# Loading the first four expert weights of each MoE layer at the end of the attention heads

## The reference

```
def hier_moe(h, w_group, b_group, w_expert, b_expert, w1, w3, w2):
    ...                      # router: one of 4 groups, 2 of its 8 experts for each token
    def expert_block(args):
        xb, e = args
        return (jax.nn.silu(xb @ w1[e]) * (xb @ w3[e])) @ w2[e]
    ...                      # each token's two results, weighed and added
```

## Time and profile before

| | us |
|---|---|
| median of 3 runs | 4473.71 |
| lowest and highest of them | 4470.65 to 4475.16 |
| the profiled execution | 4466.63 |
| its span in the profile | 4464.8 |
| TensorE busy in it | 3819.2 (86%) |
| VectorE busy | 1545.7 (35%) |
| ScalarE busy | 1355.4 (30%) |

### The profile page before, as it was taken

One profiled execution on the slowest core, in us unless ns is written; L12 is line 12 of the kernel. 1 busy time (PEld: TensorE's weight loads), 2 busy tenths in 40 slices (PEclk: granted clock), 3 DMA queues, 4 the chain that ended last, 5 costly groups with the idle time before them and its releaser, 6 DMA issues. The chain is left out here.

```text
span 4464.8 us, 76078 instructions
## 1 busy us (share of the span) xinstructions
PE 3819.2 (86%) x32246; PEld 2150.1 (48%) x32246; DVE 1545.7 (35%) x3747; ACT 1355.4 (30%) x2940; POOL 206.8 (5%) x199
## 2 busy tenths in 40 slices
PE   5999577777787699999898979989969988799997
PEld 2555366666666444666466543333335455233332
DVE  2000366666676112443236421111122183211112
ACT  2000234444433122332446422222225262222221
POOL 0000000000000000010110000000012000000000
PEclk7999789999999899999999989999979999899998
DMA  5221434343443220001210059999933000999997
GB/s 205 73 92 48 131 96 118 105 116 106 119 112 112 84 105 1 20 1 38 64 56 1 1 179 346 378 379 378 386 141 93 17 33 1 332 379 380 379 379 264
DMA packets 454316, 697.62 MB, mean 156 GB/s; under 512 B 169168, under 2 KB 195920, under 8 KB 453456
## 3 DMA queue, kind: packets, MB, share of 16 engines
q1 hardware_dynamic: 432752, 613.98, 40.0%
q0 software_dynamic: 14048, 53.49, 3.6%
q10 hardware_dynamic: 7168, 25.17, 1.4%
HBM read 625.72 MB, written 64.50 MB: 155 GB/s over the span
## 5 line engine op out<-in xcount | busy, mean ns | idle before, releaser
L200 PE MATMUL ps<-arena 128*128 128x384 f32 (+8 forms) x5516 | 1597.9, 454 | 183.2 <-issue 38.7
L200 PEld LDWEIGHTS ps<-arena 128*128 128x128 f32 (+4 forms) x5516 | 914.2, 192 | 834.6 <-issue 456.0
L2635 PE MATMUL ps<-arena 128*32 128x512 f32 x9216 | 1036.8, 603 | 50.1 <-DMA arena<-in_w 45.5
L2635 PEld LDWEIGHTS ps<-arena 128*32 128x32 f32 x9216 | 308.1, 111 | 681.0 <-issue 664.3
L576 PE MATMUL ps<-arena 64*64 64x64 f32 (+1 forms) x10624 | 459.3, 240 | 181.4 <-DVE arena L1137 65.3
L576 PEld LDWEIGHTS ps<-arena 64*64 64x64 f32 x10624 | 411.0, 145 | 260.8 <-issue 102.2
L2769 DVE COPY arena<-ps 128x384 f32<-128x384 f32 x64 | 35.7, 558 | 693.0 <-PE ps L2694 693.0
L206 PE MATMUL ps<-arena 128*128 128x128 f32 x1200 | 191.5, 295 | 82.6 <-DVE arena L3083 41.9
L2745 ACT ACTIVATE arena<-ps 96x512 f32<-96x512 f32 x64 | 38.0, 594 | 656.2 <-PE ps L2635 656.2
L206 PEld LDWEIGHTS ps<-arena 128*128 128x128 f32 x1200 | 145.6, 154 | 124.0 <-DVE arena L3083 45.3
L549 DVE SCALAR_TENSOR_TENSOR arena<-arena 128x768 f32<-128x768 f32 x48 | 45.1, 1012 | 353.3 <-PE ps L200 353.2
(11 more groups left out here) (281 smaller groups left out, 3618.8 us busy)
## 6 DMA issues: line engine op xcount, KB each, us to landing
arena<-in_w SPq DMA_DIRECT2D x192, 2048.0 KB, 22.6
arena<-in_w_mod SPq DMA_DIRECT2D x24, 2048.0 KB
arena<-in_mod_w SPq DMA_DIRECT2D x12, 2048.0 KB, 18.3
yb<-arena ACTq DMA_DIRECT2D x64, 384.0 KB, 6.3
arena<-in_rwkv_w_in SPq DMA_DIRECT2D x8, 2048.0 KB, 9.6
rkvg<-arena POOLq DMA_DIRECT2D x32, 384.0 KB, 2.6
arena<-rkvg SPq DMA_DIRECT2D x32, 384.0 KB, 3.8
arena<-di SPq DMA_DIRECT2D x192, 64.0 KB, 2.6
```

The lines of the kernel that those rows point to most:

```text
L200: ins = pe.matmul(out, l, r, start=(i == 0), stop=(i == len(pairs) - 1))
L2635: return pe.matmul(bank[32 * at:32 * at + 32, :], left[:, k, 32 * g:32 * g + 32], right[:, k, :], start=first, stop=last)
```

## The change

The ring's slots 0 to 3 become the four in the MoE's own space, and 4 and 5 become `K.slots`. The MoE's space starts at `mark + 8` (the first eight columns hold `lam`, which layer 1's output projection reads), and what the output projection reads, the heads' output `O` or `OT` and, as before, `SS`, lies beyond `mark + 20224`, past the end of the four slots. So the router's weights, the constants and weights 0 to 3 wait for the end of the heads only. Weights 4 and 5 wait for the first and second half of the output projection; weights 6 and 7 wait as before. `GA` now lies over ring slots 0 to 2. The landing semaphores are numbered so that each slot in `K.slots` keeps its own.

```
+FIRST = 20224
...
 class AbHeads:
-        self.O = K.take(KT, T)
         self.P = [[K.take(T) for _ in range(2)] for _ in range(4)]
...
         self.nsink = K.take(8)
+        K.top = max(K.top, into.mark + FIRST)
+        self.O = K.take(KT, T)
...
 class CHeads:
-        self.OT = K.take(4, D)
...
         self.SS, self.junk = K.take(4, 8), K.take(128)
+        K.top = max(K.top, into.mark + FIRST)
+        self.OT = K.take(4, D)
...
 class ExpertBlocks(Blocks):
-        self.lands = [K.land(q % RING) for q in range(len(self.order))]
+        self.lands = [K.land((q - 4) % RING) for q in range(len(self.order))]
...
 class Moe:
-        K.top = mark
+        K.top = mark + 8
...
-        self.slots = [*K.slots, *(K.take(SLOT) for _ in range(4))]
-        self.GA = [self.slots[2 + i // 4][:, 1024 * (i % 4):1024 * (i % 4) + 1024] for i in range(2 * tiles)]
+        self.slots = [*(K.take(SLOT) for _ in range(4)), *K.slots]
+        assert before.reads >= K.top
+        self.GA = [self.slots[i // 4][:, 1024 * (i % 4):1024 * (i % 4) + 1024] for i in range(2 * tiles)]
...
     def slot_free(self, e, i):
-        if i < 2:
-            e.wait_ge(*self.early[i])
+        if i < 4:
+            self.heads.over(e)
         elif i < 6:
-            self.before.over(e)
+            e.wait_ge(*self.early[i - 4])
...
     def sp(self, sp):
-        self.before.over(sp)
+        self.heads.over(sp)
         sp.dma_start(self.wr, K.I[f"router{self.layer}"].rearrange("(k p) n -> p k n", p=128)).then_inc(self.tables, 16)
```

More of the change, by code:

```diff
@@ L1991, in __init__ @@
     def __init__(self, K, mark, ahead):
-        self.K, self.s = K, K.s
+        self.K, self.s, self.mark = K, K.s, mark
         K.top = mark
@@ L2310, in __init__ @@
     def __init__(self, K, into, heads):
-        self.K, self.heads = K, heads
+        self.K, self.heads, self.reads = K, heads, into.mark + FIRST
         self.proj = OutProj(K, "ab", K.I["w_out_ab"], heads.O, K.MODS[2], 16, ((0, 0, TX), (1, TX, TC)), ((K.s["ab_mm"], 32), (K.s["ab_mm"], 32)))
@@ L2576, in __init__ @@
         self.K, self.s, self.into, self.heads = K, K.s, into, heads
+        self.reads = into.mark + FIRST
         self.O = K.take(KT, TX)
@@ L2859, with __init__ @@
 class Moe:
-    def __init__(self, K, mark, layer, before, slot_free):
-        self.K, self.s, self.layer, self.before, self.early = K, K.s, layer, before, slot_free
-        K.top = mark
+    def __init__(self, K, mark, layer, heads, before, slot_free):
+        self.K, self.s, self.layer, self.heads, self.before, self.early = K, K.s, layer, heads, before, slot_free
+        K.top = mark + 8
         self.nt = nt = T if layer == 0 else TX
@@ L3302, in second_part @@
     aout = AbOut(K, ab, heads)
-    moe = Moe(K, mark, 0, aout, ((aout.proj.done, 8), (aout.proj.done, 16)))
+    moe = Moe(K, mark, 0, heads, aout, ((aout.proj.done, 8), (aout.proj.done, 16)))
     after = TokenSums(K, "end", moe.SQ, K.carried)
@@ L3346, in third_part @@
     cout = COut(K, c, heads)
-    moe = Moe(K, mark, 1, cout, ((cout.proj.done, 4), (cout.proj.done, 8)))
+    moe = Moe(K, mark, 1, heads, cout, ((cout.proj.done, 4), (cout.proj.done, 8)))
     with K.nc.Block() as block:
```

## The result

The changed kernel took 4456.45 us in the median of 20 runs, the kernel before 4468.77 us in 20 runs beside it. The ratio is 0.9974, 95% interval [0.9965, 0.9983]. The forecast was 4466 us, a ratio of 0.9983.

What follows compares the result with a forecast made beforehand. Expert blocks are bound by transfers, anchored on block 0's first half, behind stores and first gather. Gains 4.7 - 0.1 + 5.2 - 2.1 = 7.7 us, 0.17% off the median 4473.71, give 4466.0 us; range 4458 to 4474.

Steps and rivals of the forecast that it cites:

- the base of the sum: Whole kernel: the shown median of 4473.71 us, less 0.17%, gives 4466.0 us.
- Weights 0 to 3 under the output projection, 21.5 us: Under each layer's output projection: 8.4 MB of early weights take some 21.5 us at 390 GB/s on idle engines, costing nothing.
- The last stores travel alone: Before each MoE's first gather: last token-row store lands in at most 3.5 us alone; layer 0 adds 3.9 us.
- The index is late next: Before each first gather: VectorE's index cast binds by a hair; gathers start 4.7 us (layer 0) and 5.2 us (layer 1) earlier.
- The gather, 9.5 us in both: First gather of each layer takes 9.5 us: 0.1 us lost in layer 0, 2.1 us in layer 1.
- TensorE's clock, counted as nothing: Block 0's matmuls in each layer: no change counted, 1.8 us either way for each layer.
- All behind it shifts with it: Expert blocks behind each first block, bound by transfers: they shift with the 7.7 us gain, their length unchanged.
- The rival by which the lead is kept: Expert blocks: transfers before the first block count fully, 21.5 us gained per layer, 43 us in all, 4431 us; chance 0.04.
- GpSimd's transfers late under VectorE's tensor_scalar: Last stores: data can't leave before VectorE's tensor_scalar operations end; 3.5 us of gain remain, 4470 us; chance 0.24.
- The gathers keep their 8.0 us: First gathers take 8.0 us beside weights, as in the steady flow: gain 10.7 us, 4463 us; chance 0.18.
- Slower, by TensorE under the early weights: Output projection: clock falls to 1.2 GHz for 21.5 us, 10.8 us lost per layer, 13.8 us slower, 4488 us; chance 0.09.

Runs made afterwards that it cites:

- before: The kernel before the change, unedited, in the first pair of traces: 4468.77 us in the median of 20 runs.
- same_before: The kernel before, run once more with no edit: ratio 1.0005 [0.9994, 1.0015] against itself.
- after: The changed kernel in the first pair of traces: 4456.45 us, ratio 0.9974 [0.9965, 0.9983] to the kernel before.
- same_after: The changed kernel, run once more with no edit in a second set: ratio 0.9984 [0.9976, 0.9993] to the kernel before.
- the hold: Weights 6 and 7 wait for a gather's landing: changed kernel, first gather 0.9961, third 0.9952; kernel before, first gather 0.9998.
- layout_only: Changed kernel with new places and slot order, but weights 0 to 3, router weights and constants waiting for the output projection's end: 1.0011 to the kernel before.

## Why the prediction came out as it did

The number missed its range: 4456.45 against 4458 to 4474. The step that failed is the base of the sum. "The median shown is 4473.71 ...; less 0.17% it is 4466.0" takes a median of three runs for the time of the kernel. Over 20 runs it is 4468.77, 4.9 us lower; 0.17% less of that is 4461. The range was made from the steps alone and had no term for the scatter of the base; with the same widths around the median of 20 it would have been 4453 to 4469, which holds 4456.45. The sign was there: the profiled execution, 4466.63, lay 7.1 us below the median of three. Nor is 4468.77 a fixed base, for the same kernel had medians of 4460.69 and 4464.38 in the two other sets, of 29 runs each.

Of the 9.5 us between 4466 and 4456.45 this is 4.9; the other 4.6 are the size of the effect, thus of the ratio, 0.9974 and 0.9984 against 0.9983. By the table, the fifth gather comes 7.2 us earlier in layer 0 (means of `before` and `same_before` against `after` and `same_after`) and 4.3 us in layer 1, 11.5 us together. In steps:

*Weights 0 to 3 under the output projection, 21.5 us.* They took 25 us in layer 0 (issued from 2527.54, landed at 2552.5) at 360 GB/s; nothing waits for that.

*The last stores travel alone.* Right. Forecast 3.5 us alone and about 4.4 us for the last of four, measured 3.3 and 4.6.

*The index is late next.* Right: VectorE's cast releases both gathers in the changed kernel. Forecast gains in the gather's start 4.7 and 5.2 us. Measured from the index to the gather: 5.5 to 0.9 us in layer 0, 6.0 to 0.85 us in layer 1, thus 4.6 and 5.1 us.

*The gather, 9.5 us in both.* Right in layer 1: 7.3 to 9.2 us, a loss of 1.9 us for the 2.1 that I took off. In layer 0 "0.1 us lost" was mis-sized: it became 8.4 and 8.5 us, 1.0 us gained. The prediction had weights 6 and 7 go out some 0.7 us ahead of the gather, as before; since the gather now waits for the index and they do not, the first of them went out 1.6 us (layer 0) and 1.2 us (layer 1) ahead. Why the gather is shorter in layer 0 and not in layer 1 stays open.

*TensorE's clock, counted as nothing.* Block 0's 96 matmuls in layer 0 took 12.95 and 12.84 us before (granted clock 0.81) and 11.86 and 11.82 us after (0.88 and 0.89): 1.0 us gained in each of the two pairs, though 11.9 to 12.6 us in layer 1 of the traces without the hold show nothing of the kind. `layout_only`, without early loads, took 12.54 us in layer 0, so a part of this 1.0 us may not be the change's. With the gather of layer 0 this is 2 us that the sum did not have. The rest of the 11.5 us, 1.6 us, is the index, which came 0.5 us earlier in layer 0 and 1.1 us in layer 1 in the mean of the pairs. `layout_only`, with no early load, has the early index too (30.8 us in layer 1, as `after`; 33.0 to 33.2 in `before`, `same_before` and `same_after`): chance of the clock.

So the sum of the steps as measured is 4.6 + 1.0 + 1.0 in layer 0 and 5.1 - 1.9 in layer 1, 9.8 us or 0.22%. It lies between the two ratios. The forecast of 7.7 us was 2 us short. That the second set hit the forecast ratio is luck.

*All behind it shifts with it.* Right. The stretch from the fifth gather to the last block's store is 566 to 570 us in layer 0 and 568 to 572 in layer 1 in all ten traces, early weights or not: `layout_only` has 567.6 and 569.5 us, `after` 569.5 and 570.4 us. The rival by which the lead is kept (43 us) falls with it.

*GpSimd's transfers late under VectorE's tensor_scalar.* Falls. In layer 1 of the changed kernel the last store was issued at 3818.14 and VectorE ran the eight operations over it. The timeline of VectorE:

```profile
3819.00 2.00 DVE L3185 TENSOR_SCALAR arena<-arena 128x96 f32<-128x96 f32 x8
```

The store landed in 3.3 us all the same, at 3821.4, 0.4 us behind their end; by the rival it would have been 3824. Some 0.5 MB of GpSimd's queue moved while the eight ran (3819 to 3821), so the data did leave. The gather's 0.77 us of issue stayed 0.77 as well. The rule of the Trainium skill on GpSimd's descriptors (SBUF — State Buffer, section SBUF: two separate sides) is not tested by this: the instruction that issued the store had ended at 3818.67, before the first of the eight.

*The gathers keep their 8.0 us.* Falls for layer 1. The Trainium skill's rule that the engines go round their queues packet by packet (DMA: Bandwidth & Descriptors, section Queues, rings and completion order) agrees with the trace in one thing: a gather does not stand behind all that was queued first, as weights 6 and 7, issued 1.2 and 0.7 us ahead of it, landed at 3836.0 and 3844.2 and the gather at 3832.0. That the time beside weights is the same whatever went before is not so: the first gather took 7.2 to 9.6 us beside them in the ten traces. The rival's 10.7 us lie nearer to the 9.8 us than the forecast does, but in layer 1 not by its mechanism.

*Slower, by TensorE under the early weights.* Falls. The stretch of the output projection did not grow: in layer 1, from its first matmul to VectorE's last addition, 61.12 us before (3735.89 to 3797.01) and 61.11 us after (3730.01 to 3791.12); in layer 0 91.11 us in both.

What the prediction did not look for is the loss that it priced itself. It took the gather's 9.5 us as given, beside weights that no block needed for another 30 us. Moved behind the gather, they give back about as much again as the early loads did (0.9961 against 0.9984 in one set).

## What to carry to other kernels

Where a ring of buffers is full before its first user has run, loading its first entries earlier buys nothing by itself; look for what else shared the engines with them, here the stores and the gather that the first user waits for. Send first what is waited for first. A small transfer on the path should not be issued just behind large ones that have time: the first gather, 0.39 MB, took 8.4 to 9.2 us in the changed kernel beside 4.2 MB of weights and 4.0 to 4.7 us when these were held. A change of some 0.2% can't be forecast in absolute time from three runs of a kernel whose executions scatter by 0.5%; forecast the ratio, and widen the range by the scatter of the base.

## What the runs showed of the hardware

The first indirect gather of a layer, 96 rows of 4 KB, landed in 4.0 to 4.7 us with no weights under way (two more gathers were issued 1.2 and 2.5 us behind it), in 7.2 to 9.6 us beside 2 MB loads. While three gathers and two such loads ran together (before, 2670 to 2676) the engines moved only 269 GB/s at a share of 1.05, against 380 to 420 GB/s at the same share for weights and direct stores. The router's 128x512 matmuls took 12.6 or 13.3 us in layer 0 (mean granted clock 0.83 to 0.84, or 0.79) and 8.4 or 9.2 to 9.7 us in layer 1 (0.84 or 0.72 to 0.76) in ten traces of eight programs. Kernels with and without early loads are found at either value, and in layer 1 the same program is. The index came up to 0.6 us (layer 0) and 2.4 us (layer 1) later with the longer ones: so much of any single trace can be chance.
